# Opening stage of a hybrid attention and DeltaNet block: x scaled in place by DVE, plain transposes, norm weights by their own load

## What is computed

```python
h = rms_norm(x, norm_w[l])                          # y = x * rsqrt(mean(x*x) + EPS) * w
proj = jnp.einsum('bsd,de->bse', h, w_in[l])
qa, ka, va, za, qb, kb, vb, zb, ab, bb, gate = jnp.split(proj, split_points, axis=-1)
ya = diff_attention(qa, ka, va, ...) * silu(za)
yb = rms_norm(gated_deltanet(qb, kb, vb, ab, bb, conv_w, a_log, dt_bias)) * silu(zb)
x = x + (gates[0] * (ya @ w_up_da) + gates[1] * (yb @ w_up_gdn)) @ w_out
```

## Time and profile before

| | us |
|---|---|
| median of 3 runs | 1021.48 |
| lowest, highest | 1020.8, 1021.53 |
| profiled execution, its own time | 1021.89 |
| its span, first to last instruction | 1020.2 |
| TensorE busy | 983.0 |
| DVE busy | 546.7 |
| ACT busy | 357.7 |
| POOL busy | 285.3 |

### The profile page before, as it was taken

The page is one execution under the profiler, slowest core; times in us unless marked ns, Lnnn a source line. Parts: engine busy times, 40 slices in busy tenths (PEclk is TensorE's granted clock), DMA queues, the critical chain, the costliest instruction groups (busy, mean ns, idle before and its releaser), DMA issues. The chain is left out here.

```text
span 1020.2 us, 15922 instructions
## 1 busy us (share of the span) xinstructions
PE 983.0 (96%) x5355; PEld 809.7 (79%) x5355; DVE 546.7 (54%) x1394; ACT 357.7 (35%) x773; POOL 285.3 (28%) x239
## 2 busy tenths in 40 slices
PE   7999999999999999999999999999998979999998
PEld 6888888887888888888877777777776658887887
DVE  4677776656555664566344555555555556554012
ACT  5332333433332333333235444444544542211100
POOL 4242332543223223221242223223214112222221
PEclk8999999999999999999999999999999989999999
DMA  6022122121121122021111101101110012223342
GB/s 213 22 51 51 41 51 51 33 62 54 52 62 53 32 63 63 21 73 42 32 31 32 31 21 31 31 21 31 28 24 22 21 56 73 98 72 124 124 132 105
DMA packets 70893, 56.92 MB, mean 56 GB/s; under 512 B 3298, under 2 KB 61884, under 8 KB 70844
## 3 DMA queue, kind: packets, MB, share of 16 engines
q1 hardware_dynamic: 69552, 54.15, 18.4%
q10 hardware_dynamic: 1292, 2.14, 0.7%
HBM read 48.40 MB, written 7.88 MB: 55 GB/s over the span
## 5 line engine op out<-in xcount | busy, mean ns | idle before, releaser
L1132 PE MATMUL PS<-h_hi,w_hi 128*128 128x512 f32 x784 | 318.7, 406 | 1.8 <-DVE h_lo L1537 1.4
L606 POOL TENSOR_TENSOR w_lo<-w_raw,w_hi 128x512 fp32r<-128x512 f32 x130 | 183.9, 1415 | 476.0 <-ACT w_hi L748 475.9
L1136 PE MATMUL PS<-h_hi,w_lo 128*128 128x512 f32 x784 | 314.5, 401 | 0.0
L1134 PE MATMUL PS<-h_lo,w_hi 128*128 128x512 f32 x784 | 312.2, 398 | 0.0
L1132 PEld LDWEIGHTS PS<-h_hi,w_hi 128*128 128x128 f32 x784 | 148.2, 189 | 31.0 <-DVE h_lo L1537 2.0
L1136 PEld LDWEIGHTS PS<-h_hi,w_lo 128*128 128x128 f32 x784 | 147.9, 189 | 27.7
L1134 PEld LDWEIGHTS PS<-h_lo,w_hi 128*128 128x128 f32 x784 | 148.0, 189 | 25.5
L748 ACT ACTIVATE w_hi<-w_raw 128x512 fp32r<-128x512 f32 x130 | 81.6, 629 | 196.3 <-PE PS L1136 131.5
L716 POOL TENSOR_TENSOR at_s<-at_s,neg_half 128x1 f32<-128x1 f32 x32 | 17.6, 550 | 168.7 <-DVE at_s L1909 168.7
L1041 ACT ACTIVATE prob<-PS,nm,r_qk 128x128 f32<-128x128 f32 (+7 forms) x64 | 52.6, 827 | 18.1 <-DVE nm L1878 17.7
L1596 DVE SCALAR_TENSOR_TENSOR acc<-pre,cw,acc 128x1024 f32<-128x1024 f32 x36 | 57.2, 1588 | 1.3
(11 more groups left out here) (243 smaller groups left out, 1456.8 us busy)
## 6 DMA issues: line engine op xcount, KB each, us to landing
w_raw<-in_w_in SPq DMA_DIRECT2D x98, 256.0 KB, 2.8
x_in<-in_x SPq DMA_DIRECT2D x8, 512.0 KB, 8.1
w_raw<-in_w_out SPq DMA_DIRECT2D x16, 256.0 KB, 3.2
x_res<-in_x SPq DMA_DIRECT2D x8, 512.0 KB, 4.2
out<-out_sb SPq DMA_DIRECT2D x16, 256.0 KB, 2.1
gate_dram<-gate_st SPq DMA_DIRECT2D x7, 512.0 KB, 2.9
gate_a<-gate_dram SPq DMA_DIRECT2D x7, 512.0 KB, 4.1
grow<-g_dram ACTq DMA_DIRECT2D x8, 256.0 KB, 3.3
```

The costliest lines, as they stand in the source:

```text
L606: pool.tensor_tensor(w_lo[:, b, :], w_raw[:, b, :], w_hi[:, b, :].bitcast(F32), ALU.subtract)\
L1132: pe.matmul(dst, w, hi, start=first, stop=False)
L1134: pe.matmul(dst, w, lo, start=False, stop=False)
L1136: mm = pe.matmul(dst, lo_w, hi, start=False, stop=last)
```

## The change

- ACT no longer makes diagonals, and DVE multiplies each x tile in place by row_r (scale_rows, a 128x1024 TENSOR_SCALAR). TensorE transposes the scaled x plainly with the identity (transpose_x).
- DVE squares only tile 0; ACT squares tiles 1 to 7, with the squares of tiles 4 to 7 placed ahead of pairs of round_h.
- The norm weights come by a load of their own, channel-major by a strided read, into vec[:, 48:56] on ACT's queue; the eight row loads move to SP behind the x loads.
- The transpose of vec_rows stands behind the whole first weight tile on TensorE, and channel_parameters behind all h_lo on DVE, ahead of the lambda sums.
- ACT does one small Square on the identity before there is data; WARM goes from 10 to 14.

```diff
-        WARM = 10
+        WARM = 14
...
             for t in range(NT // 2, NT):
                 load_x(t)
+            for row, rows in VEC_ROWS:
+                load_vec(row, 0, rows)
+            for row, rows in ((58, da_q_gain), (59, da_k_gain)):
+                load_vec(row, SUB, rows)
...
-            for row, src in VEC_ROWS:
-                act.dma_start(vec_rows[row:row + src.shape[0], 0:src.shape[1]], src).then_inc(vec_loaded.sem, 16)
-            for row, src in ((58, da_q_gain), (59, da_k_gain)):
-                act.dma_start(vec_rows[row:row + 1, SUB:P], src).then_inc(vec_loaded.sem, 16)
+            act.dma_start(vec[:, 48:56], norm_w[0].rearrange("(k p) -> p k", p=P), allow_slow_non_contiguous=True).then_inc(norm_loaded.sem, 16)
+            act.wait_ge(consts_ready.sem, 2)
+            act.activation(act_junk[:, :], ident[:, 0:1], ACT.Square).then_inc(table_ready.sem, 1)
...
-            square_rows(1)
-            diagonal(0)
-            diagonal(1)
-            square_rows(3)
-            diagonal(2)
-            diagonal(3)
+            for t in range(1, NT // 2):
+                if t == 3:
+                    act.wait_ge(row_sq_act.sem, row_sq_act.at(0))
+                square_rows(t)
             for b in range(2):
                 split_hi(0, b)
-            square_rows(5)
-            for n in range(NK):
-                round_h(n)
-                if n == 1:
-                    square_rows(7)
-                    diagonal(4)
-                    diagonal(5)
-                if n == 2:
-                    diagonal(6)
-                    diagonal(7)
+            for t in range(NT // 2, NT):
+                act.wait_ge(row_sq_act.sem, row_sq_act.at(t - 3))
+                square_rows(t)
+                round_h(2 * (t - NT // 2))
+                round_h(2 * (t - NT // 2) + 1)
             for n in range(NK, 2 * NK):
                 round_h(n)
...
-                return pe.matmul(PS[:, h_bank(n), (t % 4) * P:(t % 4 + 1) * P], x_in[:, t, k * P:(k + 1) * P],
-                                 diag_r[:, t, :], start=True, stop=True)
+                return pe.transpose(PS[:, h_bank(n), (t % 4) * P:(t % 4 + 1) * P], x_in[:, t, k * P:(k + 1) * P], ident[:, :])
...
-                pe.wait_ge(diag_ready.sem, diag_ready.at(NT - 1))
+                pe.wait_ge(x_scaled.sem, x_scaled.at(NT - 1))
...
             first_tile = projection(0, 0, first=True)
-            pe.wait_ge(vec_loaded.sem, 16 * (len(VEC_ROWS) + 2))
-            pe.transpose(PS[:, 7, 0:60], vec_rows[0:60, :], ident[0:60, 0:60]).then_inc(vec_T.sem, 1)
-            pe.wait_ge(consts_ready.sem, N_CONSTS)
             first_half()
             take(first_tile, 6)
             for k in range(NK):
                 take(first_tile, 3)
                 second_half(k)
             whole(first_tile)
+            pe.wait_ge(consts_ready.sem, N_CONSTS)
+            pe.wait_ge(vec_loaded.sem, 16 * (len(VEC_ROWS) + 2))
+            pe.wait_ge(h_lo_ready.sem, h_lo_ready.at(2 * NK - 1))
+            pe.transpose(PS[:, 7, 0:60], vec_rows[0:60, :], ident[0:60, 0:60]).then_inc(vec_T.sem, 1)
...
+            def scale_rows(t):
+                dve.wait_ge(row_r_ready.sem, row_r_ready.at(t))
+                dve.tensor_scalar(x_in[:, t, :], x_in[:, t, :], row_r[:, t:t + 1], None, ALU.mult).then_inc(x_scaled.sem, 1)
...
             square_rows(0)
             mean_square(0)
+            for t in range(NT // 2):
+                scale_rows(t)
+                mean_square(t + 1)
+            for n in range(NK):
+                rest_of_h(n)
+                if n % 2 == 0:
+                    scale_rows(NT // 2 + n // 2)
+                    if n < 6:
+                        mean_square(NT // 2 + 1 + n // 2)
+            for n in range(NK, 2 * NK):
+                rest_of_h(n)
             channel_parameters()
-            mean_square(1)
-            square_rows(2)
-            mean_square(2)
-            mean_square(3)
-            square_rows(4)
-            mean_square(4)
-            mean_square(5)
-            rest_of_h(0)
-            rest_of_h(1)
-            square_rows(6)
-            mean_square(6)
-            mean_square(7)
-            for n in range(2, 2 * NK):
-                rest_of_h(n)
```

More of the change, by code:

```diff
@@ L121, in hybrid_block @@
         x_in = sb(scope, "x_in", [P, NT, DM])
-        diag_r = sb(scope, "diag_r", [P, NT, P])
         row_sq = sb(scope, "row_sq", [P, NT])
@@ L125, in hybrid_block @@
         row_r = sb(scope, "row_r", [P, NT])
-        sq_junk = sb(scope, "sq_junk", [P, 2, DM])
+        sq_junk = sb(scope, "sq_junk", [P, 3, DM])
+        act_junk = sb(scope, "act_junk", [P, 1])
         scope.close()
@@ L242, in hybrid_block @@
         row_r_ready = sig("row_r_ready")
-        diag_ready = sig("diag_ready")
+        x_scaled = sig("x_scaled")
+        table_ready = sig("table_ready")
+        norm_loaded = sig("norm_loaded")
         xT_ready = sig("xT_ready")
@@ L497, in load_x, with load_vec @@
                 sp.dma_start(x_in[:, t, :], x_rows[t * P:(t + 1) * P, :]).then_inc(x_loaded[t].sem, 16)
+            def load_vec(row, col, src):
+                sp.dma_start(vec_rows[row:row + src.shape[0], col:col + src.shape[1]], src).then_inc(vec_loaded.sem, 16)
             for t in range(NT // 2):
@@ L752, in square_rows @@
                 act.wait_ge(x_loaded[t].sem, x_loaded[t].at(0))
-                act.activation(sq_junk[:, 1, :], x_in[:, t, :], ACT.Square, accum_out=row_sq[:, t:t + 1])\
+                act.activation(sq_junk[:, t % 2, :], x_in[:, t, :], ACT.Square, accum_out=row_sq[:, t:t + 1])\
                     .then_inc(row_sq_act.sem, 1)
[L755 to L759, removed]
             def round_h(n):
@@ L1103, in _, with transpose_x @@
                 pe.matmul(PS[:, n % 2, 0:P], ident[:, :], ident[:, :], start=True, stop=True)
[L1106 removed]
+            def transpose_x(t, n):
                 half, k = n // NK, n % NK
[L1109 to L1110 removed]
+                return pe.transpose(PS[:, h_bank(n), (t % 4) * P:(t % 4 + 1) * P], x_in[:, t, k * P:(k + 1) * P], ident[:, :])
             def first_half():
                 for t in range(NT // 2):
[L1114 to L1116 removed]
+                    pe.wait_ge(x_scaled.sem, x_scaled.at(t))
                     for k in range(NK):
[L1118 removed]
+                        mm = transpose_x(t, k)
                         if t == NT // 2 - 1:
@@ L1522, in square_rows @@
                 dve.wait_ge(x_loaded[t].sem, x_loaded[t].at(0))
-                dve.tensor_tensor_reduce(sq_junk[:, 0, :], x_in[:, t, :], x_in[:, t, :], 1.0, 0.0, ALU.mult, ALU.add,
+                dve.tensor_tensor_reduce(sq_junk[:, 2, :], x_in[:, t, :], x_in[:, t, :], 1.0, 0.0, ALU.mult, ALU.add,
                                          row_sq[:, t:t + 1]).then_inc(row_sq_dve.sem, 1)
-                dve.wait_ge(row_sq_dve.sem, row_sq_dve.at(t // 2))
+                dve.wait_ge(row_sq_dve.sem, row_sq_dve.at(0))
             def mean_square(t):
-                if t % 2:
-                    dve.wait_ge(row_sq_act.sem, row_sq_act.at(t // 2))
+                if t > 0:
+                    dve.wait_ge(row_sq_act.sem, row_sq_act.at(t - 1))
                 dve.tensor_scalar(row_ms[:, t:t + 1], row_sq[:, t:t + 1], 1.0 / DM, EPS, ALU.mult, ALU.add)\
                     .then_inc(row_ms_ready.sem, 1)
+            def scale_rows(t):
+                dve.wait_ge(row_r_ready.sem, row_r_ready.at(t))
+                dve.tensor_scalar(x_in[:, t, :], x_in[:, t, :], row_r[:, t:t + 1], None, ALU.mult).then_inc(x_scaled.sem, 1)
             def rest_of_h(n):
```

8 lines of the change are left out of this document (2 added, 6 removed).

## The result

The changed kernel takes 1025.99 us in the median of 5 runs (1025.14 to 1026.16), the kernel before, measured beside it, 1021.48 in the median of 5 (1019.38 to 1024.36). The ratio is 1.0045, with a 95% interval from 1.0028 to 1.0063: slower by 4.5 us, more than the 0.2% that can be told. The profiled execution took 1026.13 at a span of 1024.4, against 1021.89 at 1020.2, so the two traces differ by 4.2.

The account below looks back on a forecast made before the run. TensorE, busy 96%, was taken as the bound: its second weight tile starts 2.1 us later, plus 1.7 for low clock behind the wait, +3.8 on the 1021.48 median gives 1025.3 us, range 1022.6 to 1028.8.

Parts of the forecast that it names:

- First half worth nothing: First half of transposes ends near 13.5 instead of 19.26, priced at nothing since TensorE then waits for scaled tile 7.
- Tile 7: ACT's last square ends at 20.8, DVE has x tile 7 scaled at 23.5, against 23.02 before.
- Second half and clock: Transposes and matmuls from 23.5 take 12.3 us, plus 2.3 for low clock after idling; first tile ends at 38.1.
- The new wait: Late vector transpose and channel_parameters chain through DVE, ACT and POOL: TensorE idles 4.0 us before the second tile, formerly 0.47.
- Clock again: After the 4.0 us gap the second weight tile starts at the low clock, costing 1.7 us (bounds nothing and 3.1).
- DMAs: Strided norm load enters ACT's queue, eight row loads leave: x lands 1.9 us earlier to 1.3 later, taken as 0.
- One pass: Second half's plain transposes need one pass instead of two: 3.8 us won by the first tile's end, if the clock holds.
- the clock that stays up: Rival: TensorE's clock stays up, or falls for next to nothing, in both gaps: 1021.2 us, no change; 14%.
- Faster through earlier x: Rival: without the row loads x lands 1.9 us earlier, tile 7 is scaled at 21.6, clock holds: 1019.4 us; 6%.
- Plain transposes that don't keep the clock up: Rival: TensorE's clock stays low until the second half's transposes end, then another low stretch: 1032.4 us; 5%.
- The late norm column: Rival: strided norm weights land at 22.3, 8.4 us late for ACT's first rounding: 1033.7 us; 7%.
- Scaling in the long form: Rival: DVE's in-place scale takes 1.23 us instead of 0.75, adding 1.9 over four tiles: 1027.2 us; 8%.

Follow-up runs that it names:

- the fill: Changed kernel with 16 unread identity matmuls in one gap: ahead of the transposes' second half, 1024.16 us; or behind the vector rows' transpose, 1023.70 us.
- the kernel without the wait: Changed kernel with channel_parameters moved behind the lambda sums and 16 identity matmuls ahead of the transposes' second half: 1018.59 us.
- The two-pass kernel: Changed kernel with its transposes done as ordinary f32 matmuls by the identity, two passes a block: 1028.8 us.
- with fills: Changed kernel with 16 identity matmuls in each of two gaps, ahead of the transposes' second half and behind the vector rows' transpose: 1021.95 us.
- the hand-over out: Changed kernel with channel_parameters moved behind the lambda sums and other small DVE work, nothing left out: 1020.27 us.
- a later order: Changed kernel with channel_parameters moved late, ACT's squares and DVE's scales reordered, w_lo held until tile 3 is scaled, no extra matmuls: 1017.25 us.
- the filled kernel: Changed kernel with 16 identity matmuls between TensorE's ninth matmul and the second half of the transposes: 1024.16 us.
- the first two reordered ones: Changed kernel with channel_parameters moved late and ACT, DVE and POOL work reordered, with 6 identity matmuls (1018.65 us) and without them (1017.25 us).

## Why the prediction was right, point by point

I had forecast 1025.3 and slower; it is 1025.99 and slower. On the traces: forecast 3.8 over the profiled execution, measured 4.2. By its steps:

- **First half worth nothing.** Right. It ended at 16.0, not near 13.5 as I had put it: x tile 1 was squared 1.35 us later than before (7.22 against 5.87), a scale took 1.75, and from 12.00 TensorE had the low clock. Almost nothing hung on it: ACT's first rounding waited 0.33 us.
- **Tile 7.** Forecast 23.5 for the second half, measured 23.41; last square 20.8 forecast, 21.2 measured. The 0.4 that I added was meant for hand-overs and for POOL's w_lo; what it covered was tile 4's square at 13.0 instead of 12.7 and the 0.33 of waiting for the first half. That the sum fits this well is in part luck.
- **Second half and clock.** Forecast 12.3 us of work and 2.3 for the clock, measured 15.2 with 2.8 for the clock (5.64 / 2). The end was forecast at 38.1 and came at 38.6. The gap ahead of it was 3.5 us, not 4 to 5, since the nine matmuls themselves ran at the low clock and ended late. The clock term was 0.5 too small in the trace. At the medians, where the fill was worth 1.8, it was 0.5 too large.
- **The new wait.** Forecast 4.0 from the tile's end to the second tile, measured 3.9 (38.58 to 42.50), and 3.4 as a difference of medians, since the kernel without the wait still has 0.39 from the vector's transpose to the second tile. The five links and their order came as written.
- **Clock again.** Forecast 1.7, measured 3.38 / 2 = 1.7 in the trace, 2.3 by the fill.
- **DMAs.** Taken as 0, with up to 1.3 later. Tile 1 did land 1.35 later, but for tile 4, which heads ACT's column, the 0.3 of this trace is within what such traces differ by. The step behind the bound, 21 ns a piece, was wrong: 8.9.
- **One pass.** I put its worth at 3.8 up to the tile's end. The two-pass kernel measured 2.8. The term is 1.0 smaller at the medians; in the traces the pass count is right, but the two-pass kernel had a low stretch of 3.3 us behind its gap (23.9 to 27.2 at 0.51) where the one-pass kernel had 5.6, which gives back 1.1. So part of the difference is the clock, and not the passes.

The sum of the medians closes: +3.4 for the wait, +4.0 for the two low stretches, -2.8 for the pass, makes +4.6, measured +4.5. The wait and the clock are differences along one chain (1025.99, 1021.95, 1018.59), so what the sum tests is that the kernel with neither, plus the pass, comes out at the kernel before: 1018.59 + 2.8 is 1021.4, against 1021.5. What is left for the rest of the change (squares, scaling in place, the warm-up count) is nothing that can be told, and no run has it alone. The kernel before varies by 0.6 between the three sets of runs (1021.12 to 1021.73), and the 95% interval of a ratio reaches 0.9 to 1.8 us to each side, so no term is surer than about a microsecond.

Of the rivals, the clock that stays up fell (two stretches at 0.50; with fills it does stay up, and then the kernel comes to 1021.95, where that rival had 1021.2). Faster through earlier x fell: tile 7 came at 23.35, not 21.6; with the hand-over out, a later order that got it to 21.5 took 1017.25, against 1018.59 with tile 7 at 23.0, so an earlier tile 7 does help; the one step on the way, 21.67 with a fill behind it, gained nothing. Plain transposes that don't keep the clock up fell by the filled kernel. The late norm column fell: it landed at 5.8. Scaling in the long form fell for seven of eight tiles; the eighth took 1.0 longer, most likely for another reason, below.

## What to carry to other kernels

A step moved off the front of a list takes its wait with it, and what has to be priced is the queue behind it: here a copy of 60 columns held an exp of two, that a weight split, that a second split, and that TensorE. Move such a step behind everything that a later stage waits for, not only out of the way of the first. A gap on the engine that bounds the kernel costs twice, once as itself (3.4) and again by the slower clock behind it (1.8 to 2.3 each here); where it can't be closed, matmuls that nobody reads can keep the clock, but they pay only as long as they end before the data is there (one fill delayed the next stage by 1.7 us, another by 0.8).

## What I had not expected of the hardware

**DVE's scale and POOL's subtraction hold each other up.** A 128x1024 TENSOR_SCALAR takes 0.75 us; one that starts right behind POOL's w_lo takes 1.75: tile 3's in the changed kernel (12.19), with the first gap filled (12.16) and in every other kernel with that order, tile 4's in the first two reordered ones (14.91, 14.75). In the changed kernel w_lo began at 12.12 and takes 1.27 alone, so it ended near 13.4; the scale ended at 13.94, as if most of it had run only then. The pair of w_lo took 2.94 instead of 2 x 1.27, as if the second had waited for the scale. The other order shows as well: the w_lo that began at 42.51, 0.09 us behind a 128x1024 TENSOR_SCALAR of DVE, took 1.80. The Trainium skill (SBUF — State Buffer, Who interferes with whom) says that a tensor_scalar of DVE in a two-port mode and an operation of GpSimd share a port pair as an exclusive lock, and that the later one is blocked for the whole of the first; these rows agree. The prediction had no term for it.

**How long a low stretch lasts differs between executions of the same code.** The changed kernel and the ones with the second gap filled and with the hand-over moved have the same code up to the second half. Behind a gap of 3.54 us ahead of it the low stretch lasted 5.6 us in the first, behind 2.78 us it lasted 6.0 in the second, and behind 4.05 us 3.4 in the third, so the longer gap did not bring the longer stretch. Half of such a difference is 1.1 to 1.3 us: a clock term can't be forecast better than that, and medians and traces of one change may differ by as much.

**Small pieces slow what lands beside them, and only that.** 1024 packets of 4 bytes moved the tile that was then under way by 1.35 us (0.9 to 1.4 over the traces), and the tile three places later by nothing that can be told from the scatter. Another 1024 moved them by -0.1 and 0.25, and landed at 9.9 us after their issue instead of 5.0.
